# The opening of a one-core transformer kernel: twelve buffers for the modulation chunks, four chunks on TensorE, zero products in between, and another product order in the second half

## The chip, the cores and the metric

The kernel runs on one core of one Trainium2 chip. A core has five engines that run side by side, each with its own list of instructions: TensorE (PE) multiplies matrices into PSUM, VectorE (DVE) and ScalarE (ACT) do arithmetic between PSUM and SBUF, GpSimd (POOL) does set-up work, and SyncE (SP) issues most transfers from HBM. The engines meet at semaphores. The metric is the device time of one execution in microseconds (us), as the median of several runs.

## The reference, cut to what matters

Two blocks of two layers each act on a token matrix of 256 x 1024. Only the first sub-layer of the first layer matters here, a SwiGLU layer whose input is normalised and then modulated by vectors that are computed from `c`:

```python
cond = jax.nn.silu(c)
mod = cond @ ada_w[l] + ada_b[l]              # 1024 x 9216 weights a layer
sh1, sc1, g1, ... = jnp.split(mod, N_MOD, axis=-1)
hn = _rms_norm(h, norm_g[l, 0]) * (1 + sc1) + sh1
h = h + 0.5 * g1 * _swiglu(hn, ffn1_w_in[l], ffn1_w_out[l])
```

So nothing can be multiplied with the first layer's weights before `sh1` and `sc1` are there: 2048 columns of `ada_w[0]`, summed over 1024 rows.

## The kernel before, in words

Every float32 product is made of three: both operands are split into a rounded high part and the rest (`whi`, `wlo` for weights, `xh`, `xl` for inputs), and high x high, high x low and low x high are summed. Weights come in units of 1 MB into three buffers `raw`. For a unit ACT writes the high part (`hi`, line 1368), DVE the low part (`lo`, line 1993), PE multiplies. SP's `load` (line 405) waits until the low part of the unit three before is written, which it counts by `lo_done`.

The opening, all of it before the loops, does this:

- SP issues 16 modulation chunks of 512 KB (`ada_first`, line 415): chunk i is rows 128*(i % 8) and half f = i // 8 of the columns of shift and scale. They go round six buffers, so from chunk 6 on SP waits until the buffer's last chunk has been summed. Behind the first four chunks stands weight unit 0, behind all sixteen units 1 to 3, then a wait for the low part of unit 1, unit 4, 25 set-up loads (`setup_loads(-1)`, lines 436 to 443), unit 5, and the first tile of the next modulation (`tile_of`, line 468).
- Chunks 2, 4 and 5 are summed on PE (`mod_direct`, line 644: 8 products of a 128 x 128 block with one column), all others on DVE (`ada_first`, line 1884: one multiply-add over 128 x 1024 into `acc`, except that the first of each half only multiplies). At the end of a half PE sums `acc` over its partitions (`mod_sums`, line 668) and DVE makes shift and scale of it (`mod_columns`, line 1911).
- Between `mod_direct(2)` and `mod_direct(4)` PE turns the normalised tokens (16 transposes, line 662). ACT applies shift and scale and writes `xh` (lines 1487 and 1491), DVE writes `xl` (`rest_first`, line 1919).
- PE multiplies half the columns with weight unit f (`first_turn`, line 676): 16 products of `xh` with `wlo` and `whi` in turns, behind a wait for the low part (`split_ready`), then 8 of `xl` with `whi`. After both halves come four zero products that clear the sums (line 830), then the first group of the loop: units 2 and 3, and unit 4 (`down`), which needs `hidl`.
- On DVE the order of the opening is written out in `first` (line 2126); behind it come the products of group 0, `lo` of units 3 and 4, the sum of the first tile (`ada`, line 2158) and then `hidl` (`lower`, line 2188).

Of the kernel before, what the change touches and what calls it, by code (L numbers as in the profile page):

```python
# [6 lines left out]
ALU = mybir.AluOpType  # L7
# [8 lines left out]
P = 128  # L16
# [35 lines left out]
def program(nc, x, c, ada_w, ada_b, norm_g, ffn1_w_in, ffn1_w_out, ffn2_w_in, ffn2_w_out, w_in, w_out,  # L52
# [6 lines left out]
    KC = D // P  # L59
# [13 lines left out]
    with ExitStack() as ctx:  # L73
# [8 lines left out]
        xh = sb("xh", [P, KC, S], F32R)  # L82
# [87 lines left out]
        wsT = c1(8, P)  # L170


        adaf = arena[:, 3072:9216].rearrange("p (i t n) -> p i t n", i=6, t=2)
        accg = arena[:, 9216:10240]
        adag = arena[:, 5120:6144]
        T0 = 3072 + 2048 + 5632
# [30 lines left out]
        def sem(name):  # L207
            return ctx.enter_context(nc.semaphore(name))
# [2 lines left out]
        hi_done, lo_done, unit_used = sem("hi_done"), sem("lo_done"), sem("unit_used")  # L211
        x_loaded, c_loaded, out_stored = sem("x_loaded"), sem("c_loaded"), sem("out_stored")
        stage_loaded, smalls_loaded = sem("stage_loaded"), sem("smalls_loaded")
        ada0_loaded = [sem(f"ada0_loaded{i}") for i in range(6)]
        ada0_used = sem("ada0_used")
        adag_loaded, adag_used = sem("adag_loaded"), sem("adag_used")
        adam_loaded = [sem(f"adam_loaded{i}") for i in range(2)]
# [58 lines left out]
        def as4(t, j):  # L276
            return t[:, j, :].rearrange("p (c n) -> p c n", c=4)
# [40 lines left out]
            else:  # L318
                eng.wait_ge(acc_done, 3 * n + 2 * a + f + 1)

        ON_PE = (2, 4, 5)

        def before0(i, pe):
            return sum((k in ON_PE) == pe for k in range(i))

# [73 lines left out]
        def _(sp):  # L399
# [14 lines left out]

            def ada_first(i):

                if i >= 6:
                    sp.wait_ge(*((ada0_summed, before0(i - 5, True)) if i - 6 in ON_PE else (ada0_used, before0(i - 5, False))))
                sp.dma_start(adaf[:, i % 6], ada0[i % KC, :, i // KC, 0:2, :]).then_inc(ada0_loaded[i % 6], 16)

            def first_unit(k):

# [193 lines left out]
        def _(pe):  # L616
# [14 lines left out]
            def split_ready(L, k, i=0):  # L631
                pe.wait_ge(lo_done, L.unit(k, i) + 4)
# [4 lines left out]
            pe.wait_ge(cond_made, 1)  # L637
            pe.transpose(ps[:, 0, 0:4 * KC], cs[:, :], ident[0:4 * KC, 0:4 * KC]).then_inc(cond_turned, 1)

            def mod_columns(f):  # L640

                return [(4 * j + q, 1024 * j + 512 * f + P * q) for j in range(2) for q in range(4)]

            def mod_direct(i):

                f, k = divmod(i, KC)
                pe.wait_ge(ada0_loaded[i % 6], 16 * (i // 6 + 1))
                for at in range(KC):
                    w = adaf[:, i % 6, at // 4, P * (at % 4):P * (at % 4) + P]
                    ins = pe.matmul(ps[:, 6 + f, at:at + 1], w, condT[:, 0, k:k + 1],  # L650
                                    start=(at == 0 and i == 2), stop=False, skip_group_check=True)
                ins.then_inc(ada0_summed, 1)

            def turned0(kc):
                return ps[:, 2 + kc // 2, (kc % 2) * S:(kc % 2) * S + S]

            pe.wait_ge(cond_ready, 1)
            mod_direct(2)
            for a in range(2):
                pe.wait_ge(xs_ready, 2 * a + 2)  # L660
                for kc in range(KC):
                    ins = pe.transpose(turned0(kc)[:, a * P:a * P + P], xs[:, a, kc * P:kc * P + P], ident[:, :])
                ins.then_inc(xt_done, 2)
            mod_direct(4)
            mod_direct(5)
            pe.wait_ge(ones_ready, 1)

            def mod_sums(f):

                pe.wait_ge(ada0_used, before0(KC * f + KC, False))  # L670
                for at, col in mod_columns(f):
                    ins = pe.matmul(ps[:, 6 + f, at:at + 1], acc[:, col:col + P], ones_col[:, 0:1], start=(f == 1 and at == 0),
                                    stop=True, skip_group_check=True)
                ins.then_inc(mod_summed, 2)

            def first_turn(L):

                pe.wait_ge(minus_ready, 1)
                for f in range(2):
                    mod_sums(f)  # L680
                    split_ready(L, f)
                    wh, wl = as4(whi, f), as4(wlo, f)
                    for hh in range(2):
                        pe.wait_ge(xh_ready, 2 * f + hh + 1)
                        for a in range(2):
                            for q in (2 * hh, 2 * hh + 1):
                                kc, tok = 4 * f + q, slice(a * P, a * P + P)
                                pe.matmul(ps[:, a, :], xh[:, kc, tok], wl[:, q, :], start=(kc == 0), stop=False)
                                pe.matmul(ps[:, a, :], xh[:, kc, tok], wh[:, q, :], start=False, stop=False)
                    pe.wait_ge(x_ready, 2 * f + 2)  # L690
                    for a in range(2):
                        for q in range(4):
                            kc, tok = 4 * f + q, slice(a * P, a * P + P)
                            ins = pe.matmul(ps[:, a, :], xl[:, kc, tok], wh[:, q, :], start=False, stop=(kc == KC - 1))
                        if f == 1 and a == 0:
                            ins.then_inc(gu_ready, 1)
                    ins.then_inc(unit_used, 1)

            def turn_setup(part):

# [20 lines left out]
            def gate0(n, q):  # L721
# [6 lines left out]
                else:  # L728
                    pe.wait_ge(gate0_read, 2 * e + q)
                pe.matmul(ps[:, MB, :], ones_row[:, :], accg[:, 512 * q:512 * q + 512], start=True,  # L730
                          stop=True).then_inc(gate0_summed, 1)

            def zero_products(k):

                for _ in range(k):
                    pe.matmul(ps[:, 0, :], zerow[:, :], zerow[:, 0:1].to_broadcast([P, 512]), start=True, stop=True,
                              skip_group_check=True)

            def turn_x(n, a, f):

# [1109 lines left out]
        def _(dve):  # L1850
# [33 lines left out]
            def ada_first(i):  # L1884

                f, k = divmod(i, KC)
                dve.wait_ge(ada0_loaded[i % 6], 16 * (i // 6 + 1))
                o = acc[:, 0:2048].rearrange("p (j n) -> p j n", j=2)[:, :, 512 * f:512 * f + 512]
                if i in (0, KC):
                    ts(o, adaf[:, i % 6], condT[:, 0, k:k + 1], None, ALU.mult).then_inc(ada0_used, 1)  # L1890
                    return
                dve.wait_ge(ada0_used, before0(i, False))
                stt(o, adaf[:, i % 6], condT[:, 0, k:k + 1], o, ALU.mult, ALU.add).then_inc(ada0_used, 1)

            def first_roots():

# [229 lines left out]
            def first():  # L2126

                L = layers()[0]
                lo(L, 0)
                for i in range(6, KC + 2):  # L2130
                    ada_first(i)
                mod_columns(0)
                for i in range(KC + 2, KC + 5):
                    ada_first(i)
                rest_first(0, 0)
                ada_first(KC + 5)
                rest_first(0, 1)
                for i in (KC + 6, KC + 7):
                    ada_first(i)
                mod_columns(1)  # L2140
                dve.drain().then_inc(adam_used, 2)
                dve.drain().then_inc(adag_used, 1)
                lo(L, 1)
                for hh in range(2):
                    rest_first(1, hh)
                lo(L, 2)
# [702 lines left out]
```

## Time and profile before

| what | value |
|---|---|
| time, median of 3 runs | 2239.07 us (2237.37 to 2240.90) |
| the profiled execution | 2241.53 us, its span 2239.8 us |
| busy share of the span | PE 98%, DVE 71%, ACT 49% |
| chain that ended last | PE 88%, DVE 6%, ACT 2%, SP queue 1%, DMA 1% |
| mean granted clock | 0.998 |

The span is the time from the first to the last instruction; the run's own time holds 1.7 us more. A PE row counts from its start to a modelled end, so the distance between the starts of two rows tells better what a product costs. A releaser in brackets is what ended an engine's idle time before the row.

### The profile page before, as it was taken

How to read it: one execution, taken by the hardware profiler on the slowest of the kernel's cores; microseconds unless marked ns; L12 is line 12 of the kernel's file. 1: busy time of each engine (PE TensorE's matmuls, PEld its weight loads, DVE VectorE, ACT ScalarE, POOL GpSimd, SP SyncE). 2: the span in 40 equal slices, each digit the busy share in tenths (PEclk: the TensorE clock that was granted, in tenths of full speed). 3: DMA queues.
4: the chain of work that ended last, by engine and by line, in shares of the span. 5: the costliest groups of instructions: out<-in, count | busy, mean ns of one | idle time of the engine just before them, and what ended most of it. 6: DMA issues, size and time to landing. Idle time of an engine off the chain costs nothing.

```text
span 2239.8 us, 31962 instructions
## 1 busy us (share of the span) xinstructions
PE 2187.2 (98%) x11867; PEld 1843.9 (82%) x11867; DVE 1589.0 (71%) x1904; ACT 1097.1 (49%) x1288; POOL 52.5 (2%) x94
## 2 busy tenths in 40 slices
PE   7999999999999999999999999999999999999998
PEld 6887887887787897888788799978878879998887
DVE  5887898876777699665655778675575567867555
ACT  4344665444444466444544566554454446465443
POOL 1000010000000010000000000000000000000000
PEclk9999999999999999999999999999999999999999
DMA  8986576995687566665555464455556556435553
GB/s 283 345 315 219 162 225 209 327 315 173 242 291 244 155 212 197 229 224 192 185 190 192 154 167 132 151 188 187 187 173 203 187 169 169 133 132 170 191 191 104
DMA packets 325042, 454.56 MB, mean 203 GB/s; under 512 B 32722, under 2 KB 270040, under 8 KB 324952
## 3 DMA queue, kind: packets, MB, share of 16 engines
q1 hardware_dynamic: 320952, 440.98, 59.9%
q0 software_dynamic: 3728, 11.31, 1.7%
q8 instruction: 60, 0.98, 0.2%
q10 hardware_dynamic: 272, 1.05, 0.1%
q14 instruction: 30, 0.25, 0.0%
HBM read 449.91 MB, written 1.05 MB: 201 GB/s over the span
## 4 chain that ended last, share of the span: by engine, by line
PE 88%; DVE 6%; ACT 2%; issue 2%; DMA 1%; SPq 1%; DVEq 0%; ACTq 0%
PE ps L627 20%; PE ps L629 20%; PE ps L628 20%; PE ps L620 5%; PE ps L621 5%; PE ps L622 5%; PE ps L799 2%; DVE wlo L1993 1%; PE ps L781 1%; PE ps L784 1%; PE ps L782 1%; PE ps L718 1%; PE ps L1074 1%; ACT whi L1368 1%; DMA arena<-in_ada_w_dram 1%
## 5 line engine op out<-in xcount | busy, mean ns | idle before, releaser
L1993 DVE TENSOR_TENSOR wlo<-raw,whi 128x2048 fp32r<-128x2048 f32 x348 | 791.6, 2278 | 346.9 <-ACT whi L1368 345.4
L1368 ACT ACTIVATE whi<-raw 128x2048 fp32r<-128x2048 f32 x346 | 660.2, 1910 | 282.6 <-PE ps L629 241.5
L627 PE MATMUL ps<-whi,xl 128*128 128x512 f32 x1472 | 590.5, 401 | 0.0
L629 PE MATMUL ps<-whi,xh 128*128 128x512 f32 x1472 | 574.2, 390 | 0.0
L628 PE MATMUL ps<-wlo,xh 128*128 128x512 f32 x1472 | 574.0, 390 | 0.0
L627 PEld LDWEIGHTS ps<-whi,xl 128*128 128x128 f32 x1472 | 276.6, 188 | 61.6 <-issue 4.6
L629 PEld LDWEIGHTS ps<-whi,xh 128*128 128x128 f32 x1472 | 276.4, 188 | 60.0
L628 PEld LDWEIGHTS ps<-wlo,xh 128*128 128x128 f32 x1472 | 276.7, 188 | 57.5 <-issue 3.3
L627 PE MATMUL ps<-whi,hidl 128*128 128x512 f32 x640 | 252.1, 394 | 1.0 <-DVE hidl L2188 1.0
L620 PE MATMUL ps<-xl,whi 128*128 128x256 f32 x864 | 249.3, 288 | 1.6 <-DVE wlo L1993 1.6
L629 PE MATMUL ps<-whi,hidh 128*128 128x512 f32 x640 | 249.2, 389 | 0.0
L628 PE MATMUL ps<-wlo,hidh 128*128 128x512 f32 x640 | 249.1, 389 | 0.0
L621 PE MATMUL ps<-xh,wlo 128*128 128x256 f32 x864 | 244.4, 283 | 0.0
L622 PE MATMUL ps<-xh,whi 128*128 128x256 f32 x864 | 244.3, 283 | 0.0
L1529 ACT ACTIVATE hidh<-ps 128x512 fp32r<-128x512 f32 x80 | 47.9, 599 | 272.9 <-PE ps L799 272.9
L620 PEld LDWEIGHTS ps<-xl,whi 128*128 128x128 f32 x864 | 165.6, 192 | 4.5 <-issue 3.4
L621 PEld LDWEIGHTS ps<-xh,wlo 128*128 128x128 f32 x864 | 165.7, 192 | 1.4 <-issue 1.4
L622 PEld LDWEIGHTS ps<-xh,whi 128*128 128x128 f32 x864 | 165.6, 192 | 0.0
L2188 DVE TENSOR_TENSOR hidl<-ps,hidh 128x512 fp32r<-128x512 f32 x80 | 55.3, 691 | 142.6 <-ACT hidh L1529 142.6
L2158 DVE SCALAR_TENSOR_TENSOR arena<-arena,condT 128x1024 f32<-128x1024 f32 x104 | 133.1, 1280 | 15.9 <-DMA arena<-in_ada_w_dram 15.2
L627 PEld LDWEIGHTS ps<-whi,hidl 128*128 128x128 f32 x640 | 120.1, 188 | 27.1 <-DVE hidl L2188 1.4
L628 PEld LDWEIGHTS ps<-wlo,hidh 128*128 128x128 f32 x640 | 120.2, 188 | 25.7 <-issue 1.2
(405 smaller groups left out, 2331.6 us busy)
## 6 DMA issues: line engine op xcount, KB each, us to landing
raw<-in_ffn_w_in_dram SPq DMA_DIRECT2D x176, 512.0 KB
arena<-in_ada_w_dram SPq DMA_DIRECT2D x144, 512.0 KB, 6.0
raw<-in_w_in_dram SPq DMA_DIRECT2D x54, 1024.0 KB
raw<-in_ffn_w_out_dram SPq DMA_DIRECT2D x44, 1024.0 KB
raw<-in_w_ffn_gate_dram SPq DMA_DIRECT2D x88, 512.0 KB
raw<-in_w_ffn_up_dram SPq DMA_DIRECT2D x88, 512.0 KB
raw<-in_w_ffn_down_dram SPq DMA_DIRECT2D x44, 1024.0 KB
raw<-in_w_out_dram SPq DMA_DIRECT2D x16, 1024.0 KB
```

Source lines behind the costliest of these rows:

```text
L620: pe.matmul(o, wh, al, start=start, stop=False, **kw)
L621: pe.matmul(o, wl, ah, start=False, stop=False, **kw)
L622: return pe.matmul(o, wh, ah, start=False, stop=stop, **kw)
L627: pe.matmul(o, al, wh, start=start, stop=False, **kw)
L628: pe.matmul(o, ah, wl, start=False, stop=False, **kw)
L629: return pe.matmul(o, ah, wh, start=False, stop=stop, **kw)
L799: ins = pe.transpose(ps[:, HT, f * S + a * P:f * S + a * P + P], hid32[:, a, f * P:f * P + P], ident[:, :])
L1368: act.activation(whi[:, k % 3, :], raw[:, k % 3, :], ACT.Copy).then_inc(hi_done, 1)
L1529: act.activation(hidh[:, :, :].rearrange("p f t -> p (f t)"), ps[:, HT, :], ACT.Copy).then_inc(hidh_ready, 1)
L1993: tt(a[0], a[1], a[2].bitcast(F32), ALU.subtract).then_inc(lo_done, 1)
L2158: stt(seg, adam[:, at, :], scalar, seg, ALU.mult, ALU.add).then_inc(adam_used, 1)
L2188: tt(hidl[:, :, :].rearrange("p f t -> p (f t)"), ps[:, HT, :], hidh[:, :, :].bitcast(F32).rearrange("p f t -> p (f t)"), ALU.subtract).th ...
```

## The change

The diff does five things. The chunk buffers become twelve, four of them in `side`, `gate` and `gain`, so that SP waits only from chunk 12 on. Chunk 12 moves from DVE to PE, where it comes behind the first half's products; chunk 9 moves on DVE from before `mod_columns(0)` to behind it. PE gets zero products (a 128 x 512 product of a zero block): 7 before `mod_direct(2)`, 6 before `mod_direct(4)`, 5 behind `mod_direct(5)`, and 9 behind each `mod_sums`. In the second half the 8 products of `xh` with `whi` wait for the high part alone and come first; the 8 with `wlo` follow behind `split_ready`. The wait for `ones_ready` moves ahead.

```diff
-        adaf = arena[:, 3072:9216].rearrange("p (i t n) -> p i t n", i=6, t=2)
+        adaf = [a.rearrange("p (t n) -> p t n", t=2) for a in
+                [arena[:, at:at + 1024] for at in (3072, 4096, 5120, 6144, 7168, 8192, 12800, ARENA - 1024)]
+                + [side[:, 0:1024], gate[:, 0, :], gate[:, 1, :], gain[:, :]]]
+        NADAF = len(adaf)
...
-        ON_PE = (2, 4, 5)
+        ON_PE = (2, 4, 5, 12)
...
             def ada_first(i):
-                if i >= 6:
-                    sp.wait_ge(*((ada0_summed, before0(i - 5, True)) if i - 6 in ON_PE else (ada0_used, before0(i - 5, False))))
-                sp.dma_start(adaf[:, i % 6], ada0[i % KC, :, i // KC, 0:2, :]).then_inc(ada0_loaded[i % 6], 16)
+                if i >= NADAF:
+                    j = i - NADAF
+                    sp.wait_ge(*((ada0_summed, before0(j + 1, True)) if j in ON_PE else (ada0_used, before0(j + 1, False))))
+                sp.dma_start(adaf[i % NADAF], ada0[i % KC, :, i // KC, 0:2, :]).then_inc(ada0_loaded[i % NADAF], 16)
...
+            def zero_products(k, bank=0):
+                for _ in range(k):
+                    pe.matmul(ps[:, bank, :], zerow[:, :], zerow[:, 0:1].to_broadcast([P, 512]), start=True, stop=True,
+                              skip_group_check=True)
...
-                                    start=(at == 0 and i == 2), stop=False, skip_group_check=True)
+                                    start=(at == 0 and i in (2, 12)), stop=False, skip_group_check=True)
...
+            pe.wait_ge(ones_ready, 1)
+            zero_products(7, 1)
             pe.wait_ge(cond_ready, 1)
             mod_direct(2)
...
+            zero_products(6, 1)
             mod_direct(4)
             mod_direct(5)
-            pe.wait_ge(ones_ready, 1)
+            zero_products(5, 1)
...
                     mod_sums(f)
-                    split_ready(L, f)
+                    zero_products(9, 1 if f == 0 else 6)
                     wh, wl = as4(whi, f), as4(wlo, f)
+                    if f == 0:
+                        split_ready(L, 0)
+                    else:
+                        pe.wait_ge(hi_done, L.unit(1) + 1)
...
-                                pe.matmul(ps[:, a, :], xh[:, kc, tok], wl[:, q, :], start=(kc == 0), stop=False)
+                                if f == 0:
+                                    pe.matmul(ps[:, a, :], xh[:, kc, tok], wl[:, q, :], start=(kc == 0), stop=False)
                                 pe.matmul(ps[:, a, :], xh[:, kc, tok], wh[:, q, :], start=False, stop=False)
+                    if f == 1:
+                        split_ready(L, 1)
+                        for a in range(2):
+                            for q in range(4):
+                                pe.matmul(ps[:, a, :], xh[:, 4 + q, a * P:a * P + P], wl[:, q, :], start=False, stop=False)
...
                     ins.then_inc(unit_used, 1)
+                    if f == 0:
+                        mod_direct(12)
...
-                for i in range(6, KC + 2):
+                for i in range(6, KC + 1):
                     ada_first(i)
                 mod_columns(0)
-                for i in range(KC + 2, KC + 5):
-                    ada_first(i)
+                ada_first(KC + 1)
                 rest_first(0, 0)
-                ada_first(KC + 5)
+                ada_first(KC + 2)
                 rest_first(0, 1)
-                for i in (KC + 6, KC + 7):
+                for i in (KC + 3, KC + 5, KC + 6, KC + 7):
                     ada_first(i)
                 mod_columns(1)
```

## Rows read from the trace of the kernel before

**Rows 1.** The page, part 1: PE's busy time, share and instructions.
```profile
PE 2187.2 (98%) x11867; PEld 1843.9 (82%) x11867; DVE 1589.0 (71%) x1904; ACT 1097.1 (49%) x1288; POOL 52.5 (2%) x94
```

**Rows 2.** Waits of PE, whole run: us in total, times, longest.
```profile
PE ps L747 <- DVE u L2063: 4.6, 4, 1.6
...
PE ps L688 <- DVE wlo L1993: 3.1, 1, 3.1
...
PE ps L627 <- DVE hidl L2188: 1.0, 1, 1.0
```

**Rows 3.** Chain that ended last, first 100 us: start, us, what.
```profile
41.09 2.30 DVE wlo L1993
43.47 0.39 SPq L410
...
54.18 8.94 DMA arena<-in_ada_w_dram
...
64.55 0.69 DVE hidl L2188
65.29 0.50 PE ps L627
```

**Rows 4.** SP's queue in time: start, us, what it issued, [idle, releaser].
```profile
5.59 21.86 SPq L419 DMA_DIRECT2D arena<-in_ada_w_dram  x12
27.57 8.88 SPq L410 DMA_DIRECT2D raw<-in_ffn_w_in_dram  x6
```

**Rows 5.** Stretches: us, busy of each engine, PE clock, DMA share, GB/s.
```profile
8.00:20.00 12.00, 9.06 (x44) 9.10 (x44) 7.67 (x14) 5.12 (x7) 0.00 (x0) 1.00 1.06 379
20.00:28.00 8.00, 8.00 (x38) 7.94 (x38) 3.90 (x4) 0.00 (x0) 0.00 (x0) 1.00 0.74 236
```

**Rows 6.** PE in time, opening: start, us, instruction, shape, count, [idle, releaser].
```profile
7.03 0.28 PE L638 MATMUL ps<-ident,arena 32*128 32x32 f32 x1 [7.03 <-DVE arena L1927]
10.94 3.54 PE L650 MATMUL ps<-condT,arena 128*128 128x1 f32 x16 [3.63 <-DMA arena<-in_ada_w_dram]
14.34 3.65 PE L662 MATMUL ps<-ident,u 128*128 128x128 f32 x16
17.79 6.83 PE L650 MATMUL ps<-condT,arena 128*128 128x1 f32 x32
24.47 3.55 PE L672 MATMUL ps<-ones_col,arena 128*128 128x1 f32 x16
30.41 0.76 PE L688 MATMUL ps<-wlo,xh 128*128 128x512 f32 x1 [2.39 <-ACT xh L1491]
...
38.54 1.84 PE L672 MATMUL ps<-ones_col,arena 128*128 128x1 f32 x16
```

**Rows 7.** DVE in time: the chunk sums around the two `mod_sums`.
```profile
21.97 0.75 DVE L1890 TENSOR_SCALAR arena<-arena,condT 128x1024 f32<-128x1024 f32 x1
...
28.06 0.16 DVE L1915 SCALAR_TENSOR_TENSOR mod<-ps,condT 128x4 f32<-128x4 f32 x1 [3.52 <-PE ps L672]
...
34.78 2.67 DVE L1893 SCALAR_TENSOR_TENSOR arena<-arena,condT 128x1024 f32<-128x1024 f32 x2
```

**Rows 8.** ACT in time: the high part of unit 1.
```profile
37.98 1.91 ACT L1368 ACTIVATE whi<-raw 128x2048 fp32r<-128x2048 f32 x1 [6.14 <-DMA raw<-in_ffn_w_in_dram]
```

**Rows 9.** PE in time around 36 us: neighbouring 512-column products.
```profile
35.24 0.63 PE L689 MATMUL ps<-whi,xh 128*128 128x512 f32 x1
35.67 0.50 PE L688 MATMUL ps<-wlo,xh 128*128 128x512 f32 x1
36.00 0.39 PE L689 MATMUL ps<-whi,xh 128*128 128x512 f32 x1
36.23 0.40 PE L688 MATMUL ps<-wlo,xh 128*128 128x512 f32 x1
```

**Rows 10.** Stretches where the granted clock moves, columns as in rows 5.
```profile
42.00:43.00 1.00, 0.00 (x0) 0.00 (x0) 1.00 (x1) 1.00 (x3) 1.00 (x1) 0.85 0.17 59
...
49.00:50.00 1.00, 1.00 (x4) 0.76 (x4) 0.00 (x0) 0.00 (x0) 0.00 (x0) 0.73 0.39 76
```

More of the change, by code:

```diff
@@ L213, in program @@
         stage_loaded, smalls_loaded = sem("stage_loaded"), sem("smalls_loaded")
-        ada0_loaded = [sem(f"ada0_loaded{i}") for i in range(6)]
+        ada0_loaded = [sem(f"ada0_loaded{i}") for i in range(NADAF)]
         ada0_used = sem("ada0_used")
@@ L646, in mod_direct @@
                 f, k = divmod(i, KC)
-                pe.wait_ge(ada0_loaded[i % 6], 16 * (i // 6 + 1))
+                pe.wait_ge(ada0_loaded[i % NADAF], 16 * (i // NADAF + 1))
                 for at in range(KC):
-                    w = adaf[:, i % 6, at // 4, P * (at % 4):P * (at % 4) + P]
+                    w = adaf[i % NADAF][:, at // 4, P * (at % 4):P * (at % 4) + P]
                     ins = pe.matmul(ps[:, 6 + f, at:at + 1], w, condT[:, 0, k:k + 1],
-                                    start=(at == 0 and i == 2), stop=False, skip_group_check=True)
+                                    start=(at == 0 and i in (2, 12)), stop=False, skip_group_check=True)
                 ins.then_inc(ada0_summed, 1)
@@ L671, in mod_sums @@
                 for at, col in mod_columns(f):
-                    ins = pe.matmul(ps[:, 6 + f, at:at + 1], acc[:, col:col + P], ones_col[:, 0:1], start=(f == 1 and at == 0),
+                    ins = pe.matmul(ps[:, 6 + f, at:at + 1], acc[:, col:col + P], ones_col[:, 0:1], start=False,
                                     stop=True, skip_group_check=True)
@@ L731, in gate0 @@
                           stop=True).then_inc(gate0_summed, 1)
[L733 to L737, printed above, removed]
             def turn_x(n, a, f):
@@ L1886, in ada_first @@
                 f, k = divmod(i, KC)
-                dve.wait_ge(ada0_loaded[i % 6], 16 * (i // 6 + 1))
+                dve.wait_ge(ada0_loaded[i % NADAF], 16 * (i // NADAF + 1))
                 o = acc[:, 0:2048].rearrange("p (j n) -> p j n", j=2)[:, :, 512 * f:512 * f + 512]
                 if i in (0, KC):
-                    ts(o, adaf[:, i % 6], condT[:, 0, k:k + 1], None, ALU.mult).then_inc(ada0_used, 1)
+                    ts(o, adaf[i % NADAF], condT[:, 0, k:k + 1], None, ALU.mult).then_inc(ada0_used, 1)
                     return
                 dve.wait_ge(ada0_used, before0(i, False))
-                stt(o, adaf[:, i % 6], condT[:, 0, k:k + 1], o, ALU.mult, ALU.add).then_inc(ada0_used, 1)
+                stt(o, adaf[i % NADAF], condT[:, 0, k:k + 1], o, ALU.mult, ALU.add).then_inc(ada0_used, 1)
             def first_roots():
```

## The prediction, made before the change was run

> **What bounds the kernel now.** I read the page's busy shares first. PE is busy for 98% of the span [rows 1], so a microsecond that PE gains in the opening reaches the end, and so does one that it loses, if nothing else takes it up on the way. Then the waits of PE: after the opening the longest one anywhere is 1.6 us, and in the first groups there is a single one, 1.0 us for `hidl` [rows 2]. Then the chain of waits in the opening, which shows what that 1.0 us hides. It does not run through PE's products of the second half. It runs from the low part of unit 1 on DVE (41.09) into SP's queue (43.47: unit 4, 25 set-up loads, unit 5), from there into the first modulation tile (issued at 54.18, under way for 8.94 us), its sum on DVE, `hidl` at 64.55, and only at 65.29 back to PE [rows 3]. SP issues unit 4 as soon as that low part is written, and from there on SP, the transfers and DVE set the pace. **So the change is worth what it moves the end of unit 1's low part, 43.4 us, and nothing more.** What PE gains behind that point is lost again in front of `hidl`.
>
> Ahead of it PE is the long chain: `mod_direct(2)` from 10.94, transposes from 14.34, chunks 4 and 5 from 17.79, the first `mod_sums` from 24.47 to 28.02, the first products at 30.41, the second `mod_sums` from 38.54 to 40.38, `mod_columns`, low part [rows 3, 6].
>
> The clock decides what these cost. The 16 rows of a chunk take 3.4 us (10.94 to 14.34), and those of the first `mod_sums` 3.5 us, but the same 16 rows of the second take 1.84 us [rows 6]. Products of 512 columns start 0.43 us apart at 35.24 and 0.23 us apart at 36.0 [rows 9]. So PE ran at the lower level (1.2 GHz) from the start, through 17 us of one-column products and transposes, and rose to 2.4 GHz at 35.8, 5.4 us after the dense products began at 30.41. In the stretch 42 to 43 the granted clock is 0.85, so it fell at 42.7, 2.3 us after the last one-column product. In 49 to 50 it is 0.73, so it rose at 49.5 [rows 10], 6.1 us after lo(1) had let the products start again.
>
> **The change part by part.**
>
> *Twelve buffers.* SP's twelve issues from 5.59 last 21.9 us, since six buffers make it wait [rows 4], and from 20 to 28 the transfers run at 236 GB/s instead of 379 [rows 5]. That is 8 x 143 = 1.1 MB not moved, 3.0 us. Filled in, unit 1 lands near 35.0 instead of 37.98 [rows 8]. On the path this is worth nothing by itself: the high part of unit 1 ends at 39.9, while its low part starts at 41.09, behind `mod_columns(1)` on DVE [rows 3, 8]. If the rest gets faster by more than 4 us, the landing becomes the bound.
>
> *Chunk 12 to PE, chunk 9 behind `mod_columns(0)`.* DVE's chain between the halves keeps six chunk sums (9, 10, 11, 13, 14, 15 for 10 to 15): 28.06 to 37.45, 9.4 us [rows 7], and up to 0.6 us more, since its first `xl` waits for `xh` with one sum in front instead of three. I take 10.0. DVE saves nothing. PE gets 3.4 us at the low clock or 1.84 at the high one [rows 6], in front of the second `mod_sums`.
>
> *Zero products.* Each costs as a 512-column product, 0.43 or 0.23 us [rows 9]. The first seven (3.0 us) fit into PE's idle 3.63 us before 10.94 [rows 6]: nothing. The six and five stand where PE did not wait at all: 17.79 and 24.47 follow without a gap [rows 6]. At the low clock they cost 11 x 0.43 = 4.7 us on the path; at the high clock 11 x 0.23 = 2.5 us, against 3 x 1.6 = 4.7 us that two chunks and `mod_sums` save. The nine fill the 2.39 us before 30.41 [rows 6] at the high clock (2.1 us); at the low one they run 1.5 us over.
>
> *High parts first.* PE's 3.1 us wait for the low part of unit 1 [rows 2] goes, and 8 products of the second half run under it. The cover for what is next is the tile: PE comes 3.1 us earlier to `hidl`, and its wait there grows from 1.0 to 4.1 us. Value on the path: 0, with -3.1 us as the other end if the tile were not the bound.
>
> **The sum for the forecast.** Nothing in the trace shows what a run of zero products does to the clock, so I bound it by the two rises seen. The six zero products follow the transposes without a gap: from 14.34 that is 6 us of unbroken wide products, as long as what came before each rise (5.4 and 6.1 us). I take a rise near 19.9. Then the zero products end at 20.1, chunks 4 and 5 at 23.8 (3.7 us), five more at 25.0, `mod_sums` at 26.8 instead of 28.0: -1.2 us. DVE's sum of chunk 7, over at 22.0 [rows 7], holds nothing up. From there to the end of the second `mod_sums` it was 12.4 us (28.02 to 40.38). At the high clock PE needs 2.4 + 24 x 0.23 + 1.84 + 1.84 = 11.6 us, DVE 10.0 + 1.84 = 11.8 us; DVE's counts: -0.5 us. Unit 1's low part then ends 1.7 us earlier, and the tile, `hidl` and all that follows with it. The profiled execution took 2241.53 us, 1.7 us of them outside its span, and would take 2239.8; it lies 2.5 us above the median of the runs, 2239.07. The forecast goes by that median: 2237.4 us. Its own range is 2236.5 to 2240.
>
> That upper end is the price of a fall. The new wait of 4.1 us before `hidl` is longer than the 2.3 us after which the clock fell at 42.7 [rows 10], while 1.6 us elsewhere [rows 2] left it up. If it falls, some 13 products cost 0.20 us more until it rises again: +2.6 us. I give that 4 in 10 in every case.
>
> **The rivals.**
>
> *The zero products do not raise the clock (slower).* Then the first half stays slow to the end: 4.7 us of zero products in the path, `mod_sums(0)` ends at 32.7, nine more until 36.5, and the rise comes 5.4 us after 32.7, at 38.1, within the first half's products. These end at 42.8 (4 at 0.43, 20 at 0.23), chunk 12 at 44.6, `mod_sums(1)` at 46.6 instead of 40.4: +6.2 us, 2245.3, and 2247.9 with a fall. It decides from the point where no rise comes before 23: each chunk at the low clock costs 1.6 us. For it speaks that the transposes alone, 3.5 us, raised nothing [rows 6], and that each run of zero products (3.0, 2.6 and 2.1 us) is shorter than either run-up. Against it, that transposes and zero products together are not.
> The Trainium skill ("TensorE: Matmul & The Clock Gate", Part 4: PE-mode transpose) says that the full clock does not engage for transposes, since they are not counted as busy in the same way; by that rule this rival would hold. The trace agrees so far as it goes, but its stretch of transposes is too short to tell.
>
> *The clock rises early.* The first seven zero products run from 7.3, where PE stood idle. If the clock is up by about 14, `mod_sums(0)` is held only by DVE's chunk 7 (22.0) and ends at 23.9: -4.1, with -0.5 as above. But then unit 1, landed at 35.0, has its high part at 36.9, 0.5 us after DVE could take it. Net -4.1 us: 2235.0. For it: 3.0 us of dense products that cost nothing, and the six and five would then stand in real waits. Against: 3.0 us is half of either run-up.
>
> *The tile is not the bound.* If tile and set-up loads came through faster than seen, the 3.1 us of the second half would count too: -1.7 - 3.1, 2234.3. Against it speaks the 1.0 us wait for `hidl`, which shows the tile to be late already.
>
> **How the numbers follow.** A measurement of this kernel can tell about 0.2% (4.5 us) from no change, so faster means below 2234.6 and slower above 2243.5. Chances: forecast 0.37, no rise 0.31, early rise 0.26, tile not the bound 0.06. Slower is the first rival, 0.31. Faster is the last, and about half of the early rise, which lies 0.4 us from the border: 0.19. The rest, 0.50, is no measurable change. The range goes from 2234.0 to 2246.8: it takes in the early rise and the first rival without a fall, and leaves out that rival with one (0.31 x 0.4 = 0.12).
>
> **What would show it.** In the profile after: two starts of `mod_direct(4)` rows 0.115 us apart mean that the clock is up, 0.21 that it is not. `mod_sums(0)` should end near 26.8, unit 1's low part near 41.7, the first `hidl` near 63.5, with a PE wait of about 4 us before it. The transfers should show no dip between 20 and 28, and unit 1 should land near 35. I am wrong if PE leaves that wait much later than its low part says, if the low part of unit 1 moves by over 3 us, or if the span moves by something else than it.

## The result, and the profile after

The changed kernel takes 2243.14 us (median of 9 runs, 2241.21 to 2245.03), the kernel before 2238.55 beside it (9 runs, 2235.35 to 2241.29). The ratio is 1.0021, 95% interval [1.0012, 1.0030]: **0.2% slower, 4.6 us.** The time lies inside the range that was given, but on the other side of no change than the forecast, 2237.4. The profiled execution took 2244.53 us, its span 2242.5.

First PE in time, the opening of the changed kernel, in the columns of [rows 6]. L647 are the zero products, L660 the chunks, L674 the transposes, L685 the two `mod_sums`, L706 and L707 the first half's products.

```profile
7.04 3.17 PE L647 MATMUL ps<-zerow 128*128 128x512 bf16 x7
11.01 3.54 PE L660 MATMUL ps<-condT,arena 128*128 128x1 f32 x16 [0.80 <-DMA arena<-in_ada_w_dram]
14.42 3.65 PE L674 MATMUL ps<-ident,u 128*128 128x128 f32 x16
17.86 2.16 PE L647 MATMUL ps<-zerow 128*128 128x512 bf16 x6
19.86 4.24 PE L660 MATMUL ps<-condT,arena 128*128 128x1 f32 x32
24.34 1.91 PE L647 MATMUL ps<-zerow 128*128 128x512 bf16 x4 [0.24 <-issue]
26.05 3.41 PE L685 MATMUL ps<-ones_col,arena 128*128 128x1 f32 x16
29.32 3.86 PE L647 MATMUL ps<-zerow 128*128 128x512 bf16 x9
32.76 0.65 PE L706 MATMUL ps<-wlo,xh 128*128 128x512 f32 x1
...
38.47 1.84 PE L660 MATMUL ps<-condT,arena 128*128 128x1 f32 x16
40.18 1.93 PE L685 MATMUL ps<-ones_col,arena 128*128 128x1 f32 x16
```

The 32 rows of chunks 4 and 5 start at 19.86 and take 4.2 us instead of 6.8: the clock was up when they began, as forecast. But the 16 rows of the first `mod_sums` take 3.4 us again, the price of the lower level, and end at 29.5. The stretches of the same kernel show the moment, in the columns of [rows 5] (the third number from the end is the granted clock).

```profile
20.00:28.00 8.00, 7.76 (x47) 6.81 (x47) 2.74 (x3) 0.00 (x0) 0.00 (x0) 0.67 1.05 386
21.00:22.00 1.00, 1.00 (x11) 1.00 (x11) 1.00 (x1) 0.00 (x0) 0.00 (x0) 1.00 1.05 385
22.00:23.00 1.00, 1.00 (x10) 1.00 (x9) 0.85 (x2) 0.00 (x0) 0.00 (x0) 0.84 1.05 385
23.00:24.00 1.00, 1.00 (x6) 1.00 (x7) 0.00 (x0) 0.00 (x0) 0.00 (x0) 0.50 1.06 391
25.00:32.00 7.00, 7.00 (x26) 4.77 (x25) 1.85 (x5) 1.95 (x4) 0.00 (x0) 0.50 1.06 376
32.00:33.00 1.00, 1.00 (x5) 0.45 (x2) 1.00 (x2) 0.97 (x3) 0.00 (x0) 0.54 1.10 347
33.00:34.00 1.00, 1.00 (x6) 0.81 (x5) 1.00 (x2) 0.27 (x1) 0.00 (x0) 1.00 1.11 350
```

**The clock fell at 22.7 us**, in the middle of chunk 5, while PE was busy without a gap with one-column products, and rose only at 32.9. The five zero products, `mod_sums` and the nine zero products all ran at the low level. (Another stretch at that level, from 43.2 to 46.6 behind chunk 12 and the second `mod_sums`, slows products of the second half and lies off the path, which runs over DVE there.) The transfers, at 386 GB/s from 20 to 28, no longer dip as in [rows 5].

DVE in time, in the columns of [rows 7], shows that it was not DVE that held the first half:

```profile
22.09 0.76 DVE L1909 TENSOR_SCALAR arena<-side,condT 128x1024 f32<-128x1024 f32 x1
29.50 0.16 DVE L1934 SCALAR_TENSOR_TENSOR mod<-ps,condT 128x4 f32<-128x4 f32 x1 [6.65 <-PE ps L685]
...
35.52 4.06 DVE L1912 SCALAR_TENSOR_TENSOR arena<-arena,condT 128x1024 f32<-128x1024 f32 x3
42.14 0.16 DVE L1934 SCALAR_TENSOR_TENSOR mod<-ps,condT 128x4 f32<-128x4 f32 x1 [2.56 <-PE ps L685]
```

DVE stood idle for 6.65 us in front of `mod_columns(0)`, with chunk sums queued behind it, and after its last sum (39.6) for 2.56 us more, until PE had worked through chunk 12 and the second `mod_sums`.

Then the chain of waits, in the columns of [rows 3], which has kept its course:

```profile
42.80 2.30 DVE wlo L2012
45.19 0.39 SPq L413
...
56.44 7.35 DMA arena<-in_ada_w_dram
...
65.23 0.70 DVE hidl L2206
65.93 0.04 issue
65.97 0.50 PE ps L631
```

The low part of unit 1 ends at 45.1 instead of 43.4, and PE gets its first `hidl` product at 65.97 instead of 65.29 [rows 3]. Its wait before that has grown from 1.0 us [rows 2] to 2.5:

```profile
PE ps L631 <- DVE hidl L2206: 2.5, 1, 2.5
```

And behind this wait the clock falls once more (stretches as above):

```profile
64.00:66.00 2.00, 0.03 (x1) 0.03 (x1) 1.97 (x3) 0.36 (x2) 0.00 (x0) 1.00 1.09 381
66.00:70.00 4.00, 4.00 (x12) 3.17 (x13) 3.97 (x4) 1.91 (x1) 0.00 (x0) 0.63 1.03 409
70.00:71.00 1.00, 1.00 (x5) 0.82 (x4) 0.85 (x3) 0.00 (x0) 0.00 (x0) 0.77 1.05 414
```

From 67.0 to 70.5 eight products stand 0.43 us apart instead of 0.23, which costs 1.6 us.

### The profile page after: what moved, and what is told of

It reads as the page before. It is cut to its first block, busy times and chain, and to the rows that moved or that the text cites. A ratio compares the mean times of both kernels' runs of the same rounds, so it can differ in the third digit from the quotient of the medians.

```text
span 2242.5 us, 32051 instructions
## 1 busy us (share of the span) xinstructions
PE 2196.8 (98%) x11906; PEld 1847.2 (82%) x11919; DVE 1587.9 (71%) x1903; ACT 1096.8 (49%) x1288; POOL 52.4 (2%) x94
## 3 DMA queue, kind: packets, MB, share of 16 engines
q10 hardware_dynamic: 272, 1.05, 0.1%
HBM read 449.91 MB, written 1.05 MB: 201 GB/s over the span
## 4 chain that ended last, share of the span: by engine, by line
PE 88%; DVE 6%; ACT 2%; issue 2%; DMA 1%; SPq 1%; DVEq 0%; ACTq 0%
PE ps L631 20%; PE ps L633 20%; PE ps L632 20%; PE ps L624 5%; PE ps L625 5%; PE ps L626 5%; PE ps L818 2%; DVE wlo L2012 1%; PE ps L800 1%; PE ps L803 1%; PE ps L801 1%; PE ps L743 1%; PE ps L1093 1%; ACT whi L1387 1%; DMA arena<-in_ada_w_dram 1%
```

## The experiments

Theory A: the change is worth what it does to the low part of unit 1 and to the wait for `hidl` behind it. It costs time because chunk 12 stands in PE's path, because one-column products let the clock fall again, and because the longer wait for `hidl` lets it fall once more. Each run stands beside runs of the kernel before on the same chip (medians 2238.74, 2238.58, 2238.49 and 2239.21 in the four groups). "Changed" in the table means that the edit is made in the changed kernel, "before" that it is made in the kernel before. The rows, without the second profile of the kernel before:

| run | edit | us | ratio to before, 95% |
|---|---|---|---|
| e10 | before, twelve buffers alone | 2238.98 | 1.0004 [0.9995, 1.0013] |
| e5 | before, high parts first alone | 2238.38 | 0.9995 [0.9986, 1.0004] |
| e1 | changed, no zero products | 2240.99 | 1.0010 [1.0001, 1.0019] |
| e2 | changed, without the six and five | 2243.13 | 1.0018 [1.0009, 1.0027] |
| e11 | changed, zero products among the columns | 2242.74 | 1.0019 [1.0010, 1.0028] |
| e3 | changed, 12 more in the `hidl` wait | 2241.01 | 1.0008 [0.9999, 1.0017] |
| e4 | changed, set-up loads early | 2238.84 | 1.0003 [0.9994, 1.0012] |
| e6 | changed, chunk 12 on DVE | 2242.70 | 1.0017 [1.0008, 1.0026] |
| e9 | e6 and e3 together | 2238.99 | 1.0002 [0.9993, 1.0011] |
| e7 | before, high parts first, set-up ahead | 2237.70 | 0.9991 [0.9982, 1.0000] |
| e8 | best | 2236.02 | 0.9993 [0.9984, 1.0002] |
| e13 | before, 12 zero products later on | 2239.93 | 1.0003 [0.9994, 1.0012] |
| e15 | changed, the same 12 | 2243.24 | 1.0021 [1.0012, 1.0030] |
| e14 | best, the same 12 | 2236.03 | 0.9990 [0.9981, 0.9999] |

**Two parts alone.** Twelve buffers in the kernel before (chunks 2, 4 and 5 on PE as before, DVE's order as before):

```diff
-        adaf = arena[:, 3072:9216].rearrange("p (i t n) -> p i t n", i=6, t=2)
+        adaf = [a.rearrange("p (t n) -> p t n", t=2) for a in ...]
+        NADAF = len(adaf)
...
-                if i >= 6:
+                if i >= NADAF:
```

> The kernel before with the twelve buffers alone. Theory A: unit 1 lands near 35.0 us instead of 38.0, no dip of the transfers between 20 and 28 us, and no change of the time, since the low part of unit 1 waits for VectorE: 2238.6 within 1 us. Rival H (the twelve buffers in side, gate and gain, or the denser transfers, slow VectorE or a later transfer): 2240 or more, with chunk sums that take longer than 1.3 us.

A stretch of its trace, columns as above, to be read beside the second of [rows 5]:

```profile
20.00:28.00 8.00, 7.55 (x36) 7.46 (x35) 3.81 (x8) 0.00 (x0) 0.00 (x0) 1.00 1.05 386
```

and ACT in time, to be read beside [rows 8]:

```profile
34.01 1.91 ACT L1372 ACTIVATE whi<-raw 128x2048 fp32r<-128x2048 f32 x1 [2.65 <-DMA raw<-in_ffn_w_in_dram]
```

The transfers fill up, unit 1 lands near 34, and the time does not move. High parts first in the kernel before:

```diff
-                    split_ready(L, f)
+                    if f == 0:
+                        split_ready(L, 0)
+                    else:
+                        pe.wait_ge(hi_done, L.unit(1) + 1)
...
+                    if f == 1:
+                        split_ready(L, 1)
...
```

> The kernel before with one edit: the second half's products of xh with the high parts first, behind the high part alone. Before 2238.6. Theory A (the tile sets the end of the wait for hidl): TensorE comes some 3 us earlier to hidl and waits some 4 us there instead of 1.0; nothing gained, and where the clock falls in that wait 1.7 us lost: 2238.6 to 2240.3. Rival D (TensorE's own work sets the time): 3.1 us faster, 2235.5.

It gives 0.9995: nothing that can be told from no change. PE's 3.1 us go into the wait for `hidl`, 1.3 us in this trace. So neither of these two parts makes the change slower.

**The zero products.**

```diff
-            zero_products(7, 1)
...
-            zero_products(6, 1)
...
-            zero_products(5, 1)
...
-                    zero_products(9, 1 if f == 0 else 6)
```

> The changed kernel without any of its 36 zero products. Before 2238.55, changed 2243.14. Theory A (the changed kernel loses by chunk 12 on TensorE, 1.8 us ahead of the low part of unit 1, and by a fall of the clock in the new wait for hidl, some 1.7 us; the zero products give back in the first half what they cost): low part of unit 1 ends near 45.1 as in the changed kernel, the second half runs at the low clock, the wait for hidl shrinks to about 1 us and the clock stays up after it: 2241.5. Rival B (the zero products are the loss): 2238.5, as before.

Without any the time is 2.2 us less, near what Theory A said, but not by its way: the `hidl` wait did not shrink to 1 us. The low part of unit 1 starts at 42.59 in this trace, 0.2 us from the changed kernel's 42.80, so the gain is not there: behind a `hidl` wait of 2.4 us this execution kept its clock. Why it did, where the changed kernel lost it behind 2.5 us, stays open. Leaving out only the six and five (two lines of the same diff):

> The changed kernel without the six and five zero products around chunks 4 and 5; the seven and the nines stay. Theory A: no rise before the first mod_sums, which ends near 28.1 instead of 29.5; the nine then run at the low clock until 32 and raise it; low part of unit 1 ends 0.7 us earlier than in the changed kernel, the rest as there: 2242.5. Rival C (the rise that the six bring is worth more than they cost): slower than the changed kernel, 2244.5.

changes nothing (2243.13): nearer to what Theory A expected than to the rival, and not to be told from either Theory A or no change. The low part starts 0.7 us earlier, but the tile is under way for 8.5 us instead of 7.4, the `hidl` wait is 3.7 us, and the clock falls behind it: what the eleven products cost at the front is taken back by the tile and that wait.

Do one-column products let the clock fall? Here three zero products stand among the columns of chunk 4, of chunk 5 and of the first `mod_sums` each, and the five are left out:

```diff
                     ins = pe.matmul(ps[:, 6 + f, at:at + 1], w, condT[:, 0, k:k + 1], ...)
+                    if i in (4, 5) and at in (1, 3, 5):
+                        zero_products(1, 1)
...
-            zero_products(5, 1)
...
+                    if f == 0 and at in (1, 3, 5):
+                        zero_products(1, 1)
```

> The changed kernel with three zero products spread inside each of chunk 4, chunk 5 and the first mod_sums (behind every second column), and without the five behind chunk 5. Theory A (the clock fell at 22.7 because one-column products alone do not hold it): the granted clock stays at 1.00 from 20 to 29 us, the blocks take 1.84 + 3 x 0.23 = 2.5 us each, the first mod_sums ends near 27.7 instead of 29.5, and the time is 1 to 2 us under the changed kernel's, 2241.5. Rival I (the clock falls a few us after its rise whatever runs): low clock again from about 23 us on, mod_sums ends at 30 or later, 2243.5.

Stretches of its trace, columns as above:

```profile
20.00:24.00 4.00, 4.00 (x37) 3.86 (x37) 2.66 (x3) 0.00 (x0) 0.00 (x0) 1.00 1.05 387
24.00:25.00 1.00, 1.00 (x11) 0.94 (x11) 0.00 (x0) 0.00 (x0) 0.00 (x0) 1.00 1.06 387
25.00:26.00 1.00, 1.00 (x9) 0.91 (x7) 0.00 (x0) 0.00 (x0) 0.00 (x0) 0.57 1.11 399
```

The clock holds 2.5 us longer, to 25.1 (it had risen at 18.3, in the changed kernel at 19.3), and falls nevertheless, near the end of `mod_sums`, which ends at 26.5 instead of 29.5. That speaks for Theory A, but only in part. The rival (it falls a few us after its rise whatever runs) does not fit another trace: in e2 the clock rose at 32.9 and stayed up to 67.0. So the time since the rise does not decide it alone; what does was not tested further. The end of the run gains 0.4 us where 1 to 2 were expected: the clock is low again from 38.8, in chunk 12 and the second `mod_sums`, and behind the `hidl` wait of 1.8 us.

**The wait for `hidl`.** Twelve zero products behind the first turn, where PE waits:

```diff
                     first_turn(L)
+                    zero_products(12, 7)
```

> The changed kernel with 12 more zero products behind the first turn, ahead of the clearing of the sums: 2.8 us more work for TensorE, and the wait for hidl shorter by as much. Theory A (that wait's end is set by the tile, and the wait only costs by the fall of the clock): no fall at 67, 1.6 to 2 us faster than the changed kernel, 2241.3. Rival D (TensorE's own work sets the time there): 2.8 us slower, 2246.

Stretches of its trace, columns as above:

```profile
52.00:66.00 14.00, 13.83 (x63) 11.08 (x62) 7.59 (x5) 5.24 (x6) 0.00 (x0) 1.00 0.95 320
66.00:70.00 4.00, 4.00 (x19) 3.32 (x18) 2.84 (x6) 0.99 (x2) 0.00 (x0) 1.00 1.03 400
```

The clock stays at 1.00 behind the wait, where the changed kernel has 0.63, and the median is 2.1 us lower. By the medians this is the price of the fall. Then the other way, by taking the wait's cause away: the set-up loads go ahead of weight unit 2. (There are 23 of them in the program and in the trace, not 25 as the prediction counts.)

```diff
+            sp.wait_ge(cond_ready, 1)
+            setup_loads(-1)
             ada_chunks = ada_w.rearrange("l (c p) n -> (l c) p n", p=P)
...
-                                setup_loads(2 if i else -1)
+                                if i:
+                                    setup_loads(2)
```

> The changed kernel with the 25 set-up loads issued ahead of unit 2 instead of behind unit 4. Theory A (SP's queue, from the low part of unit 1 over the set-up loads to the first tile, sets the time at hidl): unit 1 lands some 3 us later without harm, the tile is issued near 51 instead of 56.4, no wait for hidl, no fall: 2.5 + 1.7 us faster than the changed kernel, 2239. Rival E (the tile's transfer or something behind it is the bound whatever SP does): as the changed kernel, 2243.

The first tile is issued at 50.66 instead of 56.44, there is no wait for `hidl`, no fall behind it, and the time is 2238.84: 4.3 us less. Of the 5.8 us at the tile, 2.7 are this execution's earlier low part, which starts at 40.06, and the other 3 us are SP's queue. So SP's queue carries the loss to the end, as the prediction had it.

**Chunk 12.** Back on DVE, with chunks 9 to 11 ahead of `mod_columns(0)` (in the kernel before only 9 stands there):

```diff
-        ON_PE = (2, 4, 5, 12)
+        ON_PE = (2, 4, 5)
...
-                for i in range(6, KC + 1):
+                for i in range(6, KC + 4):
                     ada_first(i)
                 mod_columns(0)
-                ada_first(KC + 1)
+                ada_first(KC + 4)
                 rest_first(0, 0)
-                ada_first(KC + 2)
                 rest_first(0, 1)
-                for i in (KC + 3, KC + 5, KC + 6, KC + 7):
+                for i in (KC + 5, KC + 6, KC + 7):
```

> The changed kernel with chunk 12 back on VectorE, and VectorE summing chunks 9, 10 and 11 ahead of mod_columns(0), where it waits 6.65 us in the changed kernel. Theory A (chunk 12 on TensorE stands on the path with 1.75 us, because TensorE and not VectorE ends the first half): low part of unit 1 ends 1.7 us earlier, 2241.4. Rival F (VectorE is the bound there, so chunk 12 on TensorE helps): slower than the changed kernel, 2244 or more.

A miss: 2242.70, only 0.4 us less. But in its trace the low part of unit 1 starts at 38.82, 4.0 us earlier than in the changed kernel. DVE sums chunks 9 to 11 there from 23.5 to 27.5, in what was its wait for `mod_sums(0)`. Not all of the 4.0 us is the edit: in this execution the clock was up from 10.1 to 13.5 as well. So it was in e3's trace, where chunk 12 is on PE. The first `mod_sums` and the low part of unit 1 there:

```profile
23.98 3.41 PE L685 MATMUL ps<-ones_col,arena 128*128 128x1 f32 x16
40.51 2.29 DVE L2013 TENSOR_TENSOR wlo<-raw,whi 128x2048 fp32r<-128x2048 f32 x1 [0.24 <-issue]
```

and in e6:

```profile
23.91 3.41 PE L685 MATMUL ps<-ones_col,arena 128*128 128x1 f32 x16
38.82 2.29 DVE L2010 TENSOR_TENSOR wlo<-raw,whi 128x2048 fp32r<-128x2048 f32 x1 [0.24 <-issue]
```

From the same `mod_sums` on, the edit gains 1.7 us, as Theory A said. The stretches of e6, columns as above, show where the gain went:

```profile
54.00:60.00 6.00, 5.05 (x23) 3.82 (x21) 0.00 (x0) 0.36 (x2) 0.00 (x0) 1.00 1.06 360
60.00:62.00 2.00, 0.00 (x0) 0.00 (x0) 0.66 (x1) 2.00 (x3) 0.00 (x0) 0.82 1.09 369
62.00:64.00 2.00, 0.72 (x2) 0.62 (x3) 2.00 (x3) 0.31 (x2) 0.00 (x0) 0.50 1.04 405
64.00:66.00 2.00, 2.00 (x6) 1.52 (x5) 1.97 (x3) 1.86 (x1) 0.00 (x0) 0.50 1.01 397
```

PE comes early, waits 4.2 us for `hidl`, and the clock falls already within the wait. This edit and the twelve zero products of e3, both diffs together, tell it apart:

> The changed kernel with chunk 12 back on VectorE (and 9 to 11 ahead of the first shift and scale, as before) and, besides, 12 zero products behind the first turn, in the wait for hidl. With chunk 12 on VectorE alone the time was 2242.7, with the zero products alone 2241.0, and the trace of the former showed a fall of the clock in a wait of 4.2 us. Theory A (chunk 12 costs 1.75 us in the path to unit 1's low part, and that gain was taken back by the fall): both together give 2241.0 - 1.75 = about 2239.3, no low clock between 58 and 70 us. Rival G (chunk 12 on PE costs nothing at the end, because the tile comes when it comes): 2241.0, as with the zero products alone.

2238.99, as Theory A said, with the clock at 1.00 from 40 to 70 us. **So by the medians the loss splits in two: 2.1 us for the fall in the `hidl` wait (2243.14 to 2241.01), 2.0 us for chunk 12 and the order of the chunks around it (to 2238.99).** What is left, 0.4 to 0.5 us, cannot be told from nothing. By the ratios to the kernel before, 1.0021, 1.0008 and 1.0002, the parts are 2.9 and 1.3 us, and each interval reaches 2 us to either side: the second part is not clear of the noise by its times alone. So the split rests on the traces as much: e3's keeps the clock that the changed kernel's loses (1.6 us there), and e6's low part is 1.7 us ahead of e3's. That e9's, at 38.32, is 2.2 us ahead of e3's shows less, since 1.9 us of it are there already when the first `mod_sums` ends (25.5 and 27.4). And how much of the 2.0 us is chunk 12 by itself stays open: it was not put back with the order of the chunks left alone, and e6 and e9 take chunks 10 and 11 ahead, which the kernel before does not.

**The kernel before, profiled again**, with no edit:

> The kernel before, profiled a second time. Its first profiled execution took 2241.5 us, 2.5 us above its median. Theory A (the opening differs from execution to execution with the moments at which the clock rises and falls): an execution nearer to the median shows an earlier rise in the opening or no fall around 42.7 us, and the low part of unit 1 ends before 43.4 us, the first hidl before 64.5. Rival J (the opening is the same and the difference lies elsewhere): the low part of unit 1 at 43.4 within 0.2 us.

Its chain of waits, columns as in [rows 3]:

```profile
40.36 2.31 DVE wlo L1993
42.74 0.39 SPq L410
53.36 7.72 DMA arena<-in_ada_w_dram
62.51 0.70 DVE hidl L2188
63.25 0.50 PE ps L627
```

This execution took 2238.86 us, and all five rows are earlier than in [rows 3], by 0.7 us at the low part and 2.0 us at `hidl`. Only 6 of the first half's products started at the lower distance, 12 in the first profile (from 30.41 in [rows 6] to 35.24 in [rows 9]), and the tile took 7.7 us instead of 8.9. Beside this one, the changed kernel's low part ends 2.4 us later, and its first product with `hidl` starts 2.7 us later. With 1.6 us for the fall that makes 4.3 us, and ACT's `hidh` rows behind it stand 4.3 to 4.4 us apart as far as 1243 us. The medians differ by 4.6. But one pair of traces cannot carry that: in the four with the changed opening (the changed kernel, e3, e4, e15) the low part of unit 1 starts between 40.06 and 42.80, in three of the kernel before's opening (its two and e13's) between 38.05 and 41.09.

**Versions that may be faster.** High parts first, with the set-up loads ahead of unit 4 so that the tile no longer binds (the diff of e5, and this one):

```diff
+                            if n == 0 and two is None and not i:
+                                sp.wait_ge(cond_ready, 1)
+                                setup_loads(-1)
                             load(L, k0 + 4, whole(as2, k0 + 4, rows2(wd, l, i, GROUPS)), i)
-                            if n == 0 and two is None:
-                                setup_loads(2 if i else -1)
+                            if n == 0 and two is None and i:
+                                setup_loads(2)
```

> The kernel before with the high parts first and with the 25 set-up loads issued ahead of unit 4, where SP stands waiting for the low part of unit 1 anyway. Theory A: the tile is issued some 6 us earlier and hidl is no longer waited for, so now the 3.1 us of the second half count and the 1.0 us of the old wait as well: 2234.5. Rival E (something behind the tile is the bound): as the kernel before, 2238.6.

and the changed kernel with the same set-up loads ahead, with chunk 12 on DVE as in e6, and of the zero products only 7, 5 and 9:

```diff
-            zero_products(6, 1)
...
-            zero_products(5, 1)
...
-                    zero_products(9, 1 if f == 0 else 6)
+                    zero_products(9 if f else 5, 6 if f else 1)
```

> What the runs so far point to: twelve buffers, chunks 9 to 11 ahead of mod_columns(0) and 12 on VectorE, zero products only where TensorE waits (seven first, five behind the first mod_sums, nine behind the second), high parts first, set-up loads ahead of unit 4. Theory A: mod_sums(0) ends at 28.1, the rise comes 1 us earlier in the first turn, low part of unit 1 ends near 42.2, first turn near 47.6 instead of 52, no wait for hidl: 2234. Rival E: as the kernel before, 2238.6.

The first gives 0.9 us instead of 4.1, a miss, and the second 2.6 instead of 4.6. The first one's trace stands 2.6 us ahead of the second profile of the kernel before at 75 us and as far ahead at 720, but 1.1 us behind at 2080. It loses that in two places, the first here (stretches, columns as above):

```profile
1270.00:1271.00 1.00, 0.99 (x7) 0.76 (x8) 0.73 (x2) 0.34 (x1) 0.00 (x0) 1.00 0.02 8
1271.00:1272.00 1.00, 0.97 (x5) 0.36 (x3) 1.00 (x1) 0.85 (x2) 0.84 (x2) 0.64 0.00 0
1272.00:1278.00 6.00, 5.97 (x26) 5.47 (x26) 2.33 (x2) 1.19 (x2) 0.21 (x1) 0.50 0.91 295
```

PE waits 1.6 us there for DVE, up to 1270.0, and behind it the clock falls, as it does in 7 of the 14 traces so far (in none of the four of the kernel before with at most one part added). Twelve zero products in that wait, in three kernels:

```diff
                 token_unit(n, k0, 1, 0)
+                for _ in range(12):
+                    pe.matmul(ps[:, 0, 0:S], zerow[:, :], zerow[:, 0:1].to_broadcast([P, S]), start=False, stop=True, ...)
                 turn_x(n, 1, 0)
```

> The kernel before with 12 zero products of 256 columns in front of the second turn of the mixing layers' first units, where PE waited 1.6 us (near 1271 and 1854 us). Theory K (the clock falls behind this wait in some executions, at 1.4 to 2.7 us each): no low clock near 1275 and 1855 us, the median 0.5 to 1.5 us lower, 2237.5, and a narrower spread. Rival L (the spread comes from the opening alone): 2238.6, spread as before. If the products themselves come late, above 2239.

> The changed kernel with the same 12 zero products in the mixing layers. Theory K: 2242, about 1 us under the changed kernel, and as far above the kernel before with these products (4.3 us by the two traces' positions at 75 us) as the opening says. Rival L: 2243.1.

> The best version so far (2236.02, eight of its runs from 2235.1 to 2236.5, three from 2239.5 to 2240.4) with the same 12 zero products. Theory K: the three high runs were falls in the mixing layers; all runs near 2235 to 2236.5, median 2235.3. Rival L: the high runs stay, median 2236.0.

The same stretches in e13, columns as above:

```profile
1271.00:1272.00 1.00, 0.75 (x8) 0.47 (x5) 1.00 (x2) 0.10 (x1) 0.00 (x0) 1.00 0.00 0
1272.00:1278.00 6.00, 5.77 (x41) 4.68 (x40) 3.71 (x3) 2.95 (x6) 1.05 (x2) 1.00 0.64 199
```

The clock is up, and so it is in all three traces. The medians of the kernel before and of the changed one do not move, so Theory K, that these later falls set the medians, is not borne out. In the best version the three high runs are gone (all 11 from 2235.37 to 2238.51) and the median is the same, 2236.03. Its interval ends just below 1: it is about 0.1% faster than the kernel before, but of fourteen intervals one that ends so near to 1 proves little. The changed kernel it beats by 7 us. Why e7 gains less in the median than its opening does stays open.

## Why the prediction was wrong, and where it was right

- **What the change is worth: right about the path, wrong in "nothing more".** The low part of unit 1, SP's queue, the tile and `hidl` carry the loss, and with the set-up loads early 4.3 us of it disappear (the same move with the high parts first in the kernel before, e7, gains 0.9 us, so not all of that need be the loss undone). But between the two profiles the low part moved by 1.7 us and the span by 2.7, which the prediction had named as a sign of being wrong: the fall behind `hidl` counts besides.
- **Twelve buffers, worth 0: right.** Unit 1's high part starts at 35.02, forecast 35.0; alone they give 1.0004.
- **The rise near 19.9: right. That the clock then stays up: wrong, and this is the step that failed first.** The zero products from 17.86 start 0.43 us apart up to 19.14 and 0.22 from 19.42 on. In all seven traces with the six zero products the clock rose before 20; but so it did in two of the ten without them, at 18.4 in e13 and 18.6 in e7, with only one-column products and transposes ahead. The sum went through chunks 4 and 5 and `mod_sums` at the high level because it had risen, and took [rows 6] at the low level as a state from the start and not as something that such products could bring back. It fell at 22.7, and `mod_sums(0)` ended at 29.5 where 26.8 was forecast: +2.7 us. The rows ahead of the prediction had a fall at 42.7, and it was put down to the idle time behind the one-column products, not to the products.
- **DVE as the bound between the halves: wrong.** From 29.46 to the end of the second `mod_sums` (42.11) it took 12.65 us, forecast 11.8: 3.3 us from `mod_sums` to the first product, 5.7 for 24 products, 1.7 for chunk 12, 1.9 for `mod_sums`. DVE's sums took the 10 us that were forecast and were done at 39.6. PE took 1.05 us more than the 11.6 it was given, 0.9 of them because the nine zero products ran at the low level (3.3 us instead of 2.4): this error hangs on the first. Chunk 12 was costed at nothing, with DVE as its cover; PE without it would have been ready at 38.5, so 0.6 of its 1.7 us lay open in this trace. DVE's end could have been earlier still, since its sums stood behind a wait of 6.65 us; with that wait used and chunk 12 on DVE the end gains 2.0 us by the medians. The two errors, 2.7 and 0.85 us, make up the difference between the forecast end of the low part, 41.7, and the measured one, 45.1.
- **High parts first, worth 0, and a longer `hidl` wait: right** (0.9995 alone; 2.5 us of wait instead of the 4.1 forecast, because PE itself came later).
- **The fall in that wait: right as a mechanism, too low in its chance, 4 in 10.** It came in the changed kernel's two traces (the second is e15's), in e2, e6 and e11, and not in e1. It cost 1.6 us in the trace and 2.1 in the medians, forecast 2.6: eight slow products, not 13. That 1.6 us leave the clock up, as the prediction read from its one trace, held in 7 of 14 traces.
- **The rivals.** That the zero products raise nothing is not what happened, though its sign is. An early rise did occur in four of the seven traces with both the seven and the six zero products (e3, e4, e6, e9, near 10 us): in that of e9 chunk 2 took 1.92 us, and `mod_sums(0)` was held by DVE's chunk 7 to 22.0, to the tenth as the rival said. But the clock fell at 20.9 and `mod_sums` took 3.4 us all the same.
- **The base of the sum.** One trace of the kernel before stood for all. Its opening is 2.0 us behind the second one's at 75 us, and that of e13, which is the same, 2.1 us ahead of it: 4.1 us between executions of the same opening, nearly the whole effect of the change. The forecast used the median for the total, which was right, but [rows 9] and [rows 10] as if the moments of rise and fall were fixed.

The Trainium skill ("TensorE: Matmul & The Clock Gate", Part 1) says that the number of slow products at the start differs from run to run of one kernel, and advises against fitting to a count. The two profiles of the kernel before agree, with 12 and 6. The Trainium skill (the same page, Part 4: PE-mode transpose) says that the full clock does not engage for transposes. The trace of e9 disagrees in so far as 16 transposes at 12.53 took 1.95 us behind an early rise, against 3.65 in [rows 6]; whether transposes alone bring the clock up no run shows.

## What to carry to other kernels

A product that keeps PE busy need not keep its clock up: before a sum is made at the high level, look at what runs next, and cost one-column products at both levels. Where an engine gains time ahead of a wait that another chain sets, the time comes back as a longer wait, and a longer wait can cost more than it gained: first shorten that chain (here 23 small loads in SP's queue), then the engine. And where the effect is as large as the spread of one opening, take two profiles of the kernel before, so that the moments of its clock aren't read as fixed.

## What the runs showed of the hardware that was not expected

- The clock fell at 22.7 us with PE busy without a gap, 2.8 us after the last zero product and 24 one-column rows into chunks 4 and 5. In e11, with zero products among them, it held to 25.1. The time since the rise does not settle it alone, since in e2 the clock stayed up from 32.9 to 67.0. In the second half the 16 rows of chunk 12 and the 16 of `mod_sums` follow each other, with nine zero products behind them: there the clock fell in four of six traces (the changed kernel, e3, e11, e15; not e2 and e4). With the 16 of `mod_sums` alone it fell in none of four (e6, e8, e9, e14).
- In or behind a wait of PE for `hidl` of 1.8 to 4.2 us the clock fell in five traces (the changed kernel, e2, e6, e11, e15: 2.5, 3.7, 4.2, 1.8 and 2.4 us) and stayed up in e1 (2.4 us); behind waits of 0.2 to 1.3 us at this place it never fell. Behind the 1.6 us near 1270 it fell in 7 of 14.
- The runs of one kernel spread over 8.7 us (the kernel before, 2235.49 to 2244.21 in the first group), and three openings of the same form alone differ by 4.1 us: 3.0 at the low part of unit 1 (41.09 and 38.05), the rest in the first tile's transfer (8.9 and 7.7 us).
- SP's 23 set-up loads take 8.9 us to issue (45.69 to 54.62 in the changed kernel), 0.39 us each, and hold the tile that stands behind them, at a cost to the end of up to 4.3 us.
